# Attention values as the stationary operand, two heads on the column halves of TensorE, and softmax scaling after the product

## The chip, the cores and the metric

The kernel runs on one NeuronCore of a Trainium2 chip. The metric is the device time of one execution in microseconds (us). The kernel before took 1717.87 us, the median of 3 runs (1717.59 to 1725.1).

## What is computed

One layer of a streaming encoder for two inputs, a prompt of 1024 tokens and a sample of 64 tokens with 512 cached ones, all in fp32. The part that matters here is the token mixer:

```python
s = (einsum("bqhd,bkhd->bhqk", qn, k_nope) + einsum("bqhd,bkd->bhqk", qr, kr_all)) * mla_scale
w = softmax(where(mask, s, -1e30), axis=-1)            # 8 latent heads ("M")
mla = einsum("bqhk,bkhd->bqhd", w, v_mla)
...
w = where(mask, exp(log_beta + after), 0)              # 4 stick-breaking heads ("S")
sb = einsum("bqhk,bkhd->bqhd", w, sv_all)
...
mix = concatenate([mla, ret, sb], axis=-1) @ w_o       # 512 + 256 + 256 columns
```

Every head has 64 value columns. `ret` are four retention heads, computed apart. Ahead of the mixer stand the modulation, the norm and the input projection; behind it the output projection, the gated MLP with its convolution and a last norm.

## The kernel before

The mixer works on nine tiles of queries: tile 0 is the sample (64 rows, five blocks of keys, the last of 64 keys), tiles 1 to 8 are the prompt (128 rows; tile n has n blocks of 128 keys). Each tile has twelve units, one per head, in the order `S0 M0 M1 S1 M2 M3 S2 M4 M5 S3 M6 M7` (`KINDS`). The program on every engine is a loop over steps, one unit per step, written out by hand, with semaphores between the engines. In step t, TensorE (`@block.tensor`) does in this order:

- `scores(t)`: query times key (L2072 for M with 96 contraction rows, L2076 for S with 64), up to 1024 columns in two PSUM banks.
- `weigh` of the unit that was transposed one step earlier (L2121): for each block of 128 keys one product, whose stationary operand is the transposed probabilities `pT` (keys x 128 queries) and whose moving operand is the values (keys x 64). The result is 128 queries x 64 value columns in PSUM.
- `transposes` of the unit two steps back (M) or five steps back (S): blocks of the probabilities are turned by TensorE (L2101), up to four to a "piece" in bank 4 or 5, and ScalarE copies each piece into `pT` (`copy_piece`, L1176). A piece waits for the copy of the piece two before it, since two banks take turns. `PIECES` and `ORDER` number the pieces.
- one of twelve steps of the `front` of the next tile (the projections of queries, keys and values, their transposes and the retention products; L1984 to L2046). Tile 8 has no front beside it.

VectorE takes the row maxima (L1603), and in `head_output` it inverts one head's row sum (L1639) and writes the scaled result into `mixtok`, the tile's rows with 1024 columns (L1641), or copies it for S (L1645). ScalarE exponentiates (L1136) and runs the four passes of the S heads (L1148 to L1156). Five steps after a tile's last unit (`MIX_STEP` 17) two pieces "X" turn all eight 128-column blocks of `mixtok` (L2092), ScalarE copies them into `mixT` (L1169), and SyncE stores the tile in one DMA of 512 KB (L724). Tile 8 is copied straight into `mix_raw`, which the output projection (L2152) reads after ScalarE and VectorE have split it into two parts (L1226, L1686).

## Time and profile before

| | |
|---|---|
| median of 3 runs | 1717.87 us |
| the profiled execution: own time / span | 1719.77 / 1718.1 us |
| TensorE busy, share of the span | 1643.7 us, 96% |
| VectorE / ScalarE / GpSimd busy | 1067.6 / 608.7 / 170.5 us |
| mean granted TensorE clock | 0.978 |
| mixer, from the first score to the first product of the output projection | about 358 to 798 us |

The span is what the profiler's records cover; the execution's own time is 1.7 us longer. Busy time of TensorE counts each product to its modelled end, so that neighbours overlap; how closely products follow one another is read from start to start. PE is TensorE's products, PEld its loads of stationary operands, DVE VectorE, ACT ScalarE, POOL GpSimd, SP SyncE. An fp32 product stands in the trace as two records, each with its own load: the program's "x7" is "x14" there. Transposes are one record.

### The profile page before, as it was taken

The numbers are of one execution on the slowest core, as the hardware profiler recorded it, in microseconds if no ns is written. First come the engines' busy times: TensorE is split into PE (matmuls) and PEld (weight loads), VectorE is DVE, ScalarE is ACT, GpSimd is POOL, SyncE is SP. The second block draws the span as 40 slices with busy tenths as digits, with TensorE's granted clock in tenths as the row PEclk, the third lists the DMA queues.
The fourth block names the chain that finished last, engine by engine and source line by source line (L and its number), as shares of the span: only waits on it lengthen the run. The fifth ranks groups of instructions, "written<-read, shape, count | busy, mean of one in ns | idle before, by whom it ended". The sixth has DMA issues, their size and how long they took to land.

```text
span 1718.1 us, 27404 instructions
## 1 busy us (share of the span) xinstructions
PE 1643.7 (96%) x9986; PEld 1483.6 (86%) x9986; DVE 1067.6 (62%) x2325; ACT 608.7 (35%) x1199; POOL 170.5 (10%) x226
## 2 busy tenths in 40 slices
PE   6899999989999999998998999999999999999996
PEld 3599999646766777778998999999999999999996
DVE  3776655447676767666236665666666666665657
ACT  4621000236566667576135222222222222222213
POOL 0011111313222221111200000000000000000000
PEclk9899999979898999999999999999999999999999
DMA  9555555511111110035101111111111111111003
GB/s 332 195 155 160 173 161 167 178 37 42 61 48 48 49 48 5 13 124 197 50 26 48 39 50 37 37 61 37 49 37 39 59 37 49 37 47 51 12 1 117
DMA packets 114221, 133.61 MB, mean 78 GB/s; under 512 B 14954, under 2 KB 91545, under 8 KB 112793
## 3 DMA queue, kind: packets, MB, share of 16 engines
q1 hardware_dynamic: 110809, 121.76, 22.2%
q0 software_dynamic: 3328, 10.73, 1.8%
q8 instruction: 53, 0.87, 0.2%
q14 instruction: 31, 0.25, 0.0%
HBM read 107.47 MB, written 27.23 MB: 78 GB/s over the span
## 4 chain that ended last, share of the span: by engine, by line
PE 87%; ACT 5%; DVE 4%; issue 3%; DMA 0%; SPq 0%; ACTq 0%; DVEq 0%
PE psum L2152 34%; PE psum L2216 15%; PE psum L1918 11%; PE psum L2121 6%; PE psum L2072 3%; PE psum L2101 3%; PE psum L2076 2%; PE psum L2004 2%; PE psum L1946 1%; PE psum L1951 1%; PE psum L1822 1%; PE psum L1984 1%; DVE h_lo L1440 1%; ACT pT L1176 1%; PE psum L1844 1%
## 5 line engine op out<-in xcount | busy, mean ns | idle before, releaser
L2152 PE MATMUL psum<-act_hi,wt_parts 128*128 128x362 f32 (+1 forms) x2496 | 614.6, 328 | 9.4 <-DVE act_lo L1440 5.2
L1758 DVE SCALAR_TENSOR_TENSOR residual<-psum,mod,residual 128x364 f32<-128x364 f32 (+2 forms) x704 | 299.5, 493 | 257.6 <-PE psum L2216 257.6
L2152 PEld LDWEIGHTS psum<-act_hi,wt_parts 128*128 128x128 f32 x2496 | 441.1, 189 | 12.1 <-issue 6.8
L2152 PE MATMUL psum<-act_lo,wt_parts 128*128 128x362 f32 (+1 forms) x1248 | 408.1, 327 | 0.0
L2216 PE MATMUL psum<-u_hi,wt_parts 128*128 128x362 f32 (+1 forms) x1056 | 263.1, 330 | 3.0 <-issue 3.0
L2152 PEld LDWEIGHTS psum<-act_lo,wt_parts 128*128 128x128 f32 x1248 | 235.2, 188 | 0.0
L2216 PEld LDWEIGHTS psum<-u_hi,wt_parts 128*128 128x128 f32 x1056 | 188.0, 189 | 3.3 <-issue 3.3
L2216 PE MATMUL psum<-u_lo,wt_parts 128*128 128x364 f32 (+1 forms) x528 | 174.5, 330 | 0.0
L1918 PE MATMUL psum<-w_hi,h_hi 128*128 128x308 f32 x512 | 158.2, 309 | 2.7 <-DVE h_lo L1440 2.1
L1918 PE MATMUL psum<-w_lo,h_hi 128*128 128x308 f32 x512 | 156.7, 306 | 0.0
L1918 PE MATMUL psum<-w_hi,h_lo 128*128 128x308 f32 x512 | 156.1, 305 | 0.0
L1278 ACT ACTIVATE u_hi<-u_val 128x362 fp32r<-128x362 f32 (+1 forms) x66 | 33.4, 508 | 291.0 <-DVE u_val L1741 291.0
L1257 ACT ACTIVATE a_ext<-psum 128x364 f32<-128x364 f32 (+1 forms) x88 | 32.1, 392 | 224.9 <-PE psum L2152 224.9
L2121 PEld LDWEIGHTS psum<-v_mla,pT 128*128 128x128 f32 (+1 forms) x656 | 80.6, 190 | 32.1 <-issue 20.1
L1650 DVE TENSOR_TENSOR wt_parts<-wt_raw,wt_parts 128x1024 fp32r<-128x1024 f32 x74 | 91.0, 1232 | 21.7 <-ACT wt_parts L1197 21.7
L1176 ACT ACTIVATE pT<-psum 128x512 f32<-128x512 f32 (+3 forms) x156 | 69.3, 476 | 98.5 <-PE psum L2101 98.3
L1918 PEld LDWEIGHTS psum<-w_hi,h_hi 128*128 128x128 f32 x512 | 97.1, 190 | 4.8 <-DVE h_lo L1440 2.5
L2216 PEld LDWEIGHTS psum<-u_lo,wt_parts 128*128 128x128 f32 x528 | 100.3, 190 | 0.0
L1918 PEld LDWEIGHTS psum<-w_hi,h_lo 128*128 128x128 f32 x512 | 96.8, 189 | 0.0
L1918 PEld LDWEIGHTS psum<-w_lo,h_hi 128*128 128x128 f32 x512 | 96.8, 189 | 0.0
L2121 PE MATMUL psum<-v_mla,pT 128*128 128x64 f32 (+1 forms) x656 | 82.1, 271 | 12.9 <-ACT pT L1176 10.5
L2072 PE MATMUL psum<-kT,qT 96*128 96x512 f32 (+4 forms) x224 | 86.4, 498 | 1.2 <-DVE zsb L1617 1.2
(236 smaller groups left out, 2221.3 us busy)
## 6 DMA issues: line engine op xcount, KB each, us to landing
wt_raw<-in_w_up SPq DMA_DIRECT2D x44, 512.0 KB, 3.9
ada_raw<-in_w_ada SPq DMA_DIRECT2D x32, 512.0 KB, 3.9
wt_raw<-in_w_down SPq DMA_DIRECT2D x22, 512.0 KB, 4.4
w_raw<-in_w_in SPq DMA_DIRECT2D x16, 616.0 KB, 5.5
z_scratch<-z_out POOLq DMA_DIRECT2D x64, 154.0 KB, 3.1
z_in<-z_scratch SPq DMA_DIRECT2D x8, 1232.0 KB, 5.3
ada_first<-in_w_ada SPq DMA_DIRECT2D x16, 512.0 KB, 11.6
xT_scratch<-xT SPq DMA_DIRECT2D x1, 4352.0 KB, 18.4
```

The costliest lines, as they stand in the source:

```text
L1176: last = act.activation(pT[:, wn % 4, :len(blocks), :r], src[:, :len(blocks), :r], ACT.Copy)\
L1278: act.activation(u_hi[:, slot, a:b], u_val[:, c % 2, :b - a], ACT.Copy).then_inc(s_uh, 1)
L1650: dve.tensor_tensor(wt_lo[:, slot], wt_raw[:, raw], wt_hi[:, slot].bitcast(F32), ALU.subtract)\
L1758: last = dve.scalar_tensor_tensor(out=res[:, d, a:b], in0=bank[4 + q % 4][:, a - CHUNKS[c][0]:b - CHUNKS[c][0]], scalar=mod[:, 40 + d, whi ...
L1918: last = pe.matmul(out[:r, 0:ZG], hh[:, k, P * t:P * t + r], ww[:, slot, k, :], start=(k == 0 and m == 0), stop=(k == KT - 1 and m == 2))
L2004: last = pe.matmul(b7[:r, 0:384], qnT[:, k, :r], w_uq[:, k, 384 * (s - 2):384 * (s - 1)], start=(k == 0), stop=(k == 2))
L2072: last = pe.matmul(out, qT[:QD, slot, h, :r], kT[:QD, h, first + a:first + b], start=True, stop=True)
L2076: last = pe.matmul(out, sqT[lo:lo + 64, slot, h // 2, :r], skT[lo:lo + 64, h // 2, first + a:first + b], start=True, stop=True)
L2101: last = pe.transpose(out[:size, P * k:P * k + r], src[:, col - first:col - first + size], ident[:r, :r])
L2121: last = pe.matmul(bank[pv_bank(v)][:r, 64 * (v % 8):64 * (v % 8) + 64], pT[:size, W_NO[x] % 4, k % 4, :r], vals, start=(k == 0), stop=(k ...
L2152: last = pe.matmul(out[:, :b - a], ww[:, slot, P * k:P * k + P], aa[:, k, a:b], start=(k == 0 and m == 0), stop=(k == KT - 1 and m == 2))
L2216: last = pe.matmul(bank[4 + q % 4][:, :b - a], ww[:, ring, P * d:P * d + P], uu[:, slot, a:b], start=(m == 0), stop=(m == 2))
```

## The change

- `plan_pairs` joins heads 2p and 2p+1 of a kind. A pair is weighed in one step, the one after its second head's transposes: the steps with a `weigh` are 2, 3, 5, 8, 9 and 11 of every twelve, six in place of twelve.
- In `weigh` the operands change places. The stationary operand is the values of one head (keys x 64 columns), the moving one `pT` (keys x 128 queries). The first head of the pair goes to PSUM partitions 0 to 63, the second to 64 to 127, block by block in turn. The result is already transposed: 128 rows (two heads) x 128 queries.
- The inverse row sum now belongs to a column, not to a partition. `invert_sums` inverts two heads' sums in one instruction; a new piece "R" of two products spreads them (stationary: the inverse broadcast to 64 columns; moving: the identity), one on each column half. ScalarE copies it to `spread`, and VectorE multiplies it into the result (`pair_output`). R stands at the end of steps 1, 4, 7 and 10 of every twelve, behind the M pieces of that step.
- `pair_output` writes straight to `mixT` (or `mix_raw` in tile 8). The pieces X shrink to the two retention blocks (`MIX_STEP` 6), and `mixtok` to 256 columns.
- `pT` has eight slots in place of four; `mixT` is stored in seven smaller DMAs per tile, each waiting for its part; `rope_a` is gone, and `oc`, `oc2`, `gate` and `junk` move in SBUF.
- The program ends two steps earlier (112 in place of 114), and ScalarE starts the split once the last pair is written.

```diff
-MIX_STEP = 17
+MIX_STEP = 6
 ADA_AT = {1: 5, 2: 5, 3: 5, 4: 5, 5: 4, 6: 4, 7: 4}
...
+def plan_pairs():
+
+    out = {}
+    for n in range(NTILE):
+        for kind, heads in (("M", H_MLA), ("S", H_SB)):
+            for h in range(0, heads, 2):
+                units = tuple(12 * n + KINDS.index((kind, x)) for x in (h, h + 1))
+                out[units[1] + T_LAG[kind] + 1] = (n, kind, h // 2, units)
+    return [(step, *out[step]) for step in sorted(out)]
+
+
+PAIRS = plan_pairs()
...
         if rest == 0 and 0 <= n < NTILE:
-            out += [("X", n, 0), ("X", n, 1)]
+            out += [("X", n, 0)]
+        if PAIR_AT.get(step + 1) in M_PAIR:
+            out += [("R", PAIR_AT[step + 1], 0)]
         steps[step] = out
     return steps
...
+            def store_pair(v):
+                _, n, kind, p, _ = PAIRS[v]
+                sp.wait_ge(s_o, v + 1)
+                if n < NTILE - 1:
+                    store_mix(n, mix_block(kind, p), 1)
...
+                if kind == "R":
+                    r, free = rows_of(PAIRS[i][1]), [v for v in M_PAIR if M_PAIR[v] == M_PAIR[i] - 2]
+                    if free:
+                        act.wait_ge(s_o, free[0] + 1)
+                    act.activation(spread[:, M_PAIR[i] % 2, :r], src[:, 0, :r], ACT.Copy).then_inc(s_pt, 1)
+                    return
+                n, slot = UNITS[i][0], piece_slot(kind, i, j)
                 r = rows_of(n)
                 blocks = key_blocks(n)[4 * j:4 * j + 4]
-                if wn >= 4:
-                    act.wait_ge(s_pv, wn - 3)
-                last = act.activation(pT[:, wn % 4, :len(blocks), :r], src[:, :len(blocks), :r], ACT.Copy)\
+                free = pair_before(n, kind, UNITS[i][2] // 2)
+                if free is not None:
+                    act.wait_ge(s_pv, free + 1)
+                last = act.activation(pT[:, slot, :len(blocks), :r], src[:, :len(blocks), :r], ACT.Copy)\
                     if blocks[-1][1] == P else None
                 if last is None:
                     if len(blocks) > 1:
-                        act.activation(pT[:, wn % 4, :len(blocks) - 1, :r], src[:, :len(blocks) - 1, :r], ACT.Copy)
-                    last = act.activation(pT[:LS, wn % 4, len(blocks) - 1, :r], src[:LS, len(blocks) - 1, :r], ACT.Copy)
+                        act.activation(pT[:, slot, :len(blocks) - 1, :r], src[:, :len(blocks) - 1, :r], ACT.Copy)
+                    last = act.activation(pT[:LS, slot, len(blocks) - 1, :r], src[:LS, len(blocks) - 1, :r], ACT.Copy)
                 last.then_inc(s_pt, 1)
 
             def split_hi(n3, raw, slot, first=False):
...
 
-            def head_output(i):
-                n, kind, h = UNITS[i]
-                r, v = rows_of(n), PV_NO[i]
-                nb = len(key_blocks(n))
-                o = bank[pv_bank(v)][:r, 64 * (v % 8):64 * (v % 8) + 64]
+            def invert_sums(v):
+
+                _, n, kind, p, units = PAIRS[v]
+                r, u = rows_of(n), count_units("M", units[0])
+                dve.wait_ge(s_p, u + 2)
+                dve.reciprocal(inverse[:r, (u // 2) % 2, :], rowsum[:r, u % 4:u % 4 + 2, 0]).then_inc(s_nd, 1)
+
+            def pair_output(v):
+
+                _, n, kind, p, _ = PAIRS[v]
+                r, b = rows_of(n), mix_block(kind, p)
+                dve.wait_ge(s_pv, v + 1)
+                if n == NTILE - 1:
+                    dve.wait_ge(s_ret, NTILE)
+                    dve.wait_ge(s_fp, 12 * NTILE)
+                    dve.wait_ge(s_fA, read_a(NTILE, 0))
+                    out = mix_raw[:, b, LP - P:LP]
+                else:
+                    if n:
+                        dve.wait_ge(block_stored(b), 16 * n)
+                    out = mixT[:, b, :r]
+                result = bank[pv_bank(v)][:, P * (v % 4):P * (v % 4) + r]
                 if kind == "M":
-                    j = count_units("M", i)
-                    dve.wait_ge(s_p, j + 1)
-                    ch.link(dve.reciprocal(rowsum[:r, j % 4, 1:2], rowsum[:r, j % 4, 0:1]))
-                    dve.wait_ge(s_pv, W_NO[kind, i, (nb + 3) // 4 - 1] + 1)
-                    dve.tensor_scalar(mixtok[:r, n % 2, 64 * h:64 * h + 64], o, rowsum[:r, j % 4, 1:2], None,
-                                      ALU.mult).then_inc(s_o, 1)
+                    pieces_done(dve, ("R", v, 0))
+                    dve.tensor_tensor(out, result, spread[:, M_PAIR[v] % 2, :r], ALU.mult).then_inc(s_o, 1)
                 else:
-                    dve.wait_ge(s_pv, W_NO[kind, i, (nb + 3) // 4 - 1] + 1)
-                    dve.tensor_copy(mixtok[:r, n % 2, 768 + 64 * h:832 + 64 * h], o).then_inc(s_o, 1)
+                    dve.tensor_copy(out, result).then_inc(s_o, 1)
 
             def split_lo(n3, raw, slot):
 
...
                 if 0 <= step < len(UNITS):
                     (row_max if UNITS[step][1] == "M" else stick_logits)(step)
-                for x in PIECES.get(step - 1, []):
-                    if x[0] != "X" and x[2] == 0:
-                        head_output(x[1])
+                if step in PAIR_AT:
+                    pair_output(PAIR_AT[step])
                 if 0 <= step - 2 < len(UNITS) and UNITS[step - 2][1] == "S":
                     stick_sums(step - 2)
                 if s == 0 and 0 < m <= NTILE:
...
-                        pe.wait_ge(s_o, 12 * (i + 1))
-                    for k in range(4):
-                        last = pe.transpose(out[:, P * k:P * k + r],
-                                            mixtok[:r, i % 2, P * (4 * j + k):P * (4 * j + k) + P], ident[:r, :r])
+                    pe.wait_ge(s_ret, i + 1)
+                    for k in range(2):
+                        last = pe.transpose(out[:, P * k:P * k + r], mixtok[:r, i % 2, P * k:P * k + P], ident[:r, :r])
+                elif kind == "R":
+                    r, m = rows_of(PAIRS[i][1]), M_PAIR[i]
+                    pe.wait_ge(s_nd, m + 1)
+                    for a in range(2):
+                        last = pe.matmul(out[64 * a:64 * a + 64, 0:r], inverse[:r, m % 2, a:a + 1].broadcast_to([r, 64]),
+                                         ident[:r, :r], start=True, stop=True)
                 else:
                     n = UNITS[i][0]
                     r, u = rows_of(n), count_units(kind, i)
-                    pe.wait_ge(s_p if kind == "M" else s_w, u + 1)
+                    if kind == "M":
...
                     pe.wait_ge(s_sv, 80 if n < 5 else 96)
                 blocks = key_blocks(n)
                 for k, (_, size, tile_) in enumerate(blocks):
-                    x = (kind, i, k // 4)
                     if k % 4 == 0:
-                        pieces_done(pe, x)
-                    vals = v_mla[:size, tile_, 64 * h:64 * h + 64] if kind == "M" else \
-                        sv[:size, tile_, 64 * h:64 * h + 64]
-                    last = pe.matmul(bank[pv_bank(v)][:r, 64 * (v % 8):64 * (v % 8) + 64], pT[:size, W_NO[x] % 4, k % 4, :r],
-                                     vals, start=(k == 0), stop=(k == len(blocks) - 1))
-                    if k % 4 == 3 or k == len(blocks) - 1:
-                        last.then_inc(s_pv, 1)
+                        pieces_done(pe, (kind, units[0], k // 4))
+                        pieces_done(pe, (kind, units[1], k // 4))
+                    for a, i in enumerate(units):
+                        h = UNITS[i][2]
+                        vals = v_mla[:size, tile_, 64 * h:64 * h + 64] if kind == "M" else \
+                            sv[:size, tile_, 64 * h:64 * h + 64]
+                        last = pe.matmul(bank[pv_bank(v)][64 * a:64 * a + 64, P * (v % 4):P * (v % 4) + r], vals,
+                                         pT[:size, piece_slot(kind, i, k // 4), k % 4, :r],
+                                         start=(k == 0), stop=(k == len(blocks) - 1))
+                last.then_inc(s_pv, 1)
 
             for step in range(-12, STEPS):
                 m, s = divmod(step + 12, 12)
                 if 0 <= step < len(UNITS):
                     scores(step)
-                for x in PIECES.get(step - 1, []):
-                    if x[0] != "X" and x[2] == 0:
-                        weigh(x[1])
+                if step in PAIR_AT:
+                    weigh(PAIR_AT[step])
                 for x in PIECES.get(step, []):
                     transposes(x)
                 if m == 0:
```

TensorE in tile 4 (four blocks of keys), its steps 1 and 2: scores of M0 and M1, and what stands between them, before:

```order
L2072 MATMUL psum<-kT,qT 128x512 [waits softmax_exp_written]
L2121 MATMUL psum<-v_mla,pT 128x64 [waits piece_copied,head_output_written]
L2121 MATMUL psum<-v_mla,pT 128x64 x3
L2101 MATMUL psum<-ident_sb,prob 128x128 [waits softmax_exp_written,piece_copied]
L2101 MATMUL psum<-ident_sb,prob 128x128 x3
L2004 MATMUL psum<-w_uq_sb,qnT 128x384 [waits front_bank_read_by_scalar,front_bank_read_by_vector]
L2004 MATMUL psum<-w_uq_sb,qnT 128x384 x2
L2072 MATMUL psum<-kT,qT 128x512 [waits stick_logits_copied]
L2121 MATMUL psum<-v_mla,pT 128x64 [waits piece_copied,head_output_written]
L2121 MATMUL psum<-v_mla,pT 128x64 x3
```

The same two steps now (L2153 are the scores, L2210 `weigh`, L2189 the transposes, L2176 the piece R, L2085 the front's product with `w_uq`):

```order
L2153 MATMUL psum<-kT,qT 128x512 [waits softmax_exp_written]
L2189 MATMUL psum<-ident_sb,prob 128x128 [waits softmax_exp_written,piece_copied]
L2189 MATMUL psum<-ident_sb,prob 128x128 x3
L2176 MATMUL psum<-ident_sb,inverse 64x128 [waits pair_row_sums_inverted,piece_copied]
L2176 MATMUL psum<-ident_sb,inverse 64x128
L2085 MATMUL psum<-w_uq_sb,qnT 128x384 [waits front_bank_read_by_scalar,front_bank_read_by_vector]
L2085 MATMUL psum<-w_uq_sb,qnT 128x384 x2
L2153 MATMUL psum<-kT,qT 128x512 [waits stick_logits_copied]
L2210 MATMUL psum<-pT,v_mla 64x128 [waits piece_copied,head_pair_written]
L2210 MATMUL psum<-pT,v_mla 64x128 x7
L2189 MATMUL psum<-ident_sb,esb 128x128 [waits stick_weights_written,piece_copied]
L2189 MATMUL psum<-ident_sb,esb 128x128 x3
```

The four products of one head in each step are gone; eight products of two heads stand in the second step only, and the two of R stand between the transposes and the front in the first.

The last steps of TensorE's mixer (tile 8), before:

```order
L2072 MATMUL psum<-kT,qT 128x512 x2
L2121 MATMUL psum<-v_mla,pT 128x64 x8
L2101 MATMUL psum<-ident_sb,esb 128x128 x8
L2121 MATMUL psum<-sv,pT 128x64 x8
L2101 MATMUL psum<-ident_sb,prob 128x128 x8
L2121 MATMUL psum<-v_mla,pT 128x64 x8
L2101 MATMUL psum<-ident_sb,prob 128x128 x8
L2121 MATMUL psum<-v_mla,pT 128x64 x8
L2101 MATMUL psum<-ident_sb,esb 128x128 x8
L2121 MATMUL psum<-sv,pT 128x64 x8
L2092 MATMUL psum<-ident_sb,mixtok 128x128 x8
```

and now:

```order
L2176 MATMUL psum<-ident_sb,inverse 64x128 x2
L2153 MATMUL psum<-kT,qT 128x512 x2
L2210 MATMUL psum<-pT,v_mla 64x128 x16
L2189 MATMUL psum<-ident_sb,esb 128x128 x8
L2189 MATMUL psum<-ident_sb,prob 128x128 x16
L2176 MATMUL psum<-ident_sb,inverse 64x128 x2
L2210 MATMUL psum<-pT,v_mla 64x128 x16
L2189 MATMUL psum<-ident_sb,esb 128x128 x8
L2210 MATMUL psum<-pT,sv 64x128 x16
```

The closing transposes of `mixtok` are gone. Behind the last scores, five `weigh` of one head each have become three of a pair.

## Rows read from the trace of the kernel before

**Rows 1.** The page, parts 1 and 2: busy time, and the 40 slices of the span.

```profile
PE 1643.7 (96%) x9986; PEld 1483.6 (86%) x9986; DVE 1067.6 (62%) x2325; ACT 608.7 (35%) x1199; POOL 170.5 (10%) x226
...
PE   6899999989999999998998999999999999999996
...
PEclk9899999979898999999999999999999999999999
```

**Rows 2.** Windows: tiles 1, 4 and 7, first score to first score of the next.

```profile
core 0: us, PE busy (x) PEld busy (x) DVE busy (x) ACT busy (x) POOL busy (x), PEclk, DMA share, GB/s
407.60:436.60 29.00, 25.91 (x188) 20.00 (x187) 23.04 (x83) 19.05 (x71) 10.01 (x16) 1.00 0.20 63
...
512.60:560.30 47.70, 44.91 (x240) 32.25 (x239) 32.03 (x87) 29.59 (x68) 11.70 (x15) 0.89 0.13 43
...
665.70:726.60 60.90, 59.70 (x373) 45.39 (x372) 40.51 (x85) 40.21 (x74) 10.19 (x7) 1.00 0.03 10
```

**Rows 3.** Waits of PE, 366 to 800 us: total us, times, longest.

```profile
PE psum L2121 <- ACT pT L1176: 11.2, 16, 1.4
...
PE psum L2092 <- ACT pT L1176: 1.9, 5, 0.6
PE psum L2121 <- DVE mixtok L1641: 1.8, 1, 1.8
```

**Rows 4.** Timeline of PE in tile 7: start us, us, instruction, count.

```profile
704.84 0.60 PE L1984 MATMUL psum<-ident_sb,qtok 128*96 128x128 f32 x4
705.28 1.67 PE L2072 MATMUL psum<-kT,qT 96*128 96x512 f32 x4
706.78 1.67 PE L2121 MATMUL psum<-v_mla,pT 128*128 128x64 f32 x14
708.29 0.93 PE L2101 MATMUL psum<-ident_sb,esb 128*128 128x128 f32 x7
709.06 0.60 PE L1984 MATMUL psum<-ident_sb,qtok 128*96 128x128 f32 x4
709.59 1.77 PE L2076 MATMUL psum<-skT,sqT 64*128 64x512 f32 x4
711.29 1.77 PE L2121 MATMUL psum<-sv,pT 128*128 128x64 f32 x14
712.90 0.93 PE L2101 MATMUL psum<-ident_sb,prob 128*128 128x128 f32 x7
```

**Rows 5.** The same stretch, loads of stationary operands, around the S scores.

```profile
709.59 0.29 PEld L2076 LDWEIGHTS psum<-skT,sqT 64*128 64x128 f32 x2 [0.18 <-issue]
...
711.29 1.64 PEld L2121 LDWEIGHTS psum<-sv,pT 128*128 128x128 f32 x14 [0.54 <-issue]
```

**Rows 6.** Timeline of PEld in tile 0, 389.17 to 389.56 us: loads 64 wide.

```profile
389.10 0.55 PEld L2121 LDWEIGHTS psum<-v_mla,pT 128*64 128x64 f32 x8
```

**Rows 7.** Groups of the mixer, 358 to 797 us: count, busy us, mean ns, idle.

```profile
L1641 DVE TENSOR_SCALAR mixtok<-psum,rowsum 128x64 f32<-128x64 f32 (+1 forms) x72 | 20.4, 283 | 13.2 <-PE psum L2121 10.5 <-DVE rowsum L1639 0.2
...
L1639 DVE RECIPROCAL rowsum<-rowsum 128x1 f32<-128x1 f32 (+1 forms) x72 | 10.9, 152 | 0.0
...
L1645 DVE COPY mixtok<-psum 128x64 f32<-128x64 f32 (+1 forms) x36 | 7.7, 213 | 5.4 <-PE psum L2121 5.4
```

**Rows 8.** Timeline of the mixer's end.

```profile
792.63 1.97 PE L2121 MATMUL psum<-sv,pT 128*128 128x64 f32 x16 [0.34 <-ACT pT L1176]
794.63 0.23 DVE L1645 COPY mixtok<-psum 128x64 f32<-128x64 f32 x1 [2.83 <-PE psum L2121]
...
795.67 1.08 ACT L1169 ACTIVATE mix_raw<-psum 128x512 f32<-128x512 f32 x2 [2.70 <-PE psum L2092]
...
796.87 1.30 ACT L1226 ACTIVATE act_hi<-mix_raw 128x364 fp32r<-128x364 f32 x3
```

**Rows 9.** Windows at the lower clock, in tile 0 and in tile 4.

```profile
363.20:380.30 17.10, 15.96 (x49) 8.04 (x50) 7.75 (x15) 8.18 (x19) 2.84 (x3) 0.50 0.27 90
...
520.20:530.50 10.30, 10.30 (x36) 7.35 (x36) 6.29 (x13) 5.36 (x14) 1.27 (x1) 0.50 0.35 133
```

More of the change, by code:

```diff
@@ L222 @@
 PIECE_NO = {x: q for q, x in enumerate(ORDER)}
[L223 to L227 removed]
 PV_LAST_LOW, PV_FIRST_TAIL = 12 * 5 - 2, 12 * 8 + 1
 def pv_bank(v):
[L233 to L234 removed]
+    step, _, kind, _, _ = PAIRS[v]
+    if kind == "S" and 12 <= step <= PV_LAST_LOW:
         return 1
[L236 removed]
+    if kind == "S" and step >= PV_FIRST_TAIL:
         return 7
@@ L1134, in softmax_exp @@
                 if j >= 4:
[L1135 removed]
+                    act.wait_ge(s_nd, (j - 4) // 2 + 1)
                 act.activation(prob[:r, j % 3, :w], score_bank(i, w)[:r], ACT.Exp, bias=maxes[:r, j % 2, 1:2],
@@ L2100, in transposes, with weigh @@
                     for k, (col, size, _) in enumerate(key_blocks(n)[4 * j:4 * j + 4]):
-                        last = pe.transpose(out[:size, P * k:P * k + r], src[:, col - first:col - first + size],
-                                            ident[:r, :r])
+                        to, of = out[:size, P * k:P * k + r], src[:, col - first:col - first + size]
+                        last = pe.transpose(to, of, ident[:r, :r])
                 last.then_inc(s_tr, 1)
-            def weigh(i):
-                n, kind, h = UNITS[i]
-                r, v = rows_of(n), PV_NO[i]
+            def weigh(v):
+                _, n, kind, p, units = PAIRS[v]
+                r = rows_of(n)
                 if pv_user_before(v, pv_bank(v)) is not None:
```

117 lines of the change are left out of this document (72 added, 45 removed).

## The prediction

> **What bounds the kernel now.** I read the page first: TensorE is busy 96% of the span, and only a few of the forty slices fall under 9 tenths [rows 1]. The change touches the mixer alone, 358 to 798 us, so I cut that into its tiles. Tile 7 takes 60.9 us with PE busy 59.7 and no DMA to speak of; ScalarE is busy 40.2 and VectorE 40.5 of them. Tile 4 has PE busy 44.9 of 47.7, tile 1 25.9 of 29.0 [rows 2]. TensorE bounds the large tiles; in the small ones part of the time is a chain of engines answering each other. The named waits of PE in the whole mixer are small, 11.2 us for ScalarE's copies being the largest [rows 3]. So the question is what the new order costs TensorE, product by product.
>
> **How dear a `weigh` is.** In tile 7, with seven blocks, the M scores start at 705.28 and 706.78 is the first of the values' products, 708.29 the first transpose: 1.51 us for 14 records [rows 4], 0.108 us a record, 0.216 a block and head. The seven transposes behind it take 0.77 us, 0.110 each [rows 4]. A product streams 64 columns there and a transpose 128, yet both follow at the same pace, so the 128-wide load sets it. Scores of 896 columns take 1.50 us in two passes: 0.84 us per 1000 columns and pass, so 128 fp32 columns stream in 0.107. A load 64 wide is cheaper: in tile 0 eight of them span 0.55 us, and with a single record of 0.14 taken off, seven intervals of 0.058 [rows 6].
>
> **How dear a change of tile shape is.** The S scores use 64 contraction rows, the M scores 96. Against the M case, the step ahead of the S scores is longer by 0.09 (709.06 to 709.59 beside 704.84 to 705.28), the scores themselves by 0.20 (1.70 beside 1.50) and the values behind by 0.10 (1.61 beside 1.51) [rows 4]: 0.39 us for going to the half array and back. The load records say why: the first load behind each change starts with its product, and is not hidden under the one before [rows 5]. I take 0.20 us a change where a 128-wide load follows, and 0.15 where the load is 64 wide (0.20 less 0.110, plus 0.058). The Trainium skill, TensorEngine Tiling (Array Packing), Key Properties, says that changing the tiling mode drains TensorE; by that rule, the trace agrees. It speaks against this change, which puts two changes around every new `weigh` and every R.
>
> **The sum on TensorE.**
>
> 1. *Products with the values.* Twelve heads in tiles 1 to 8 have 1+2+...+8 = 36 blocks each: 216 pairs of blocks at 2 x 0.216 = 0.432 us. Now each is four records of 128 streamed columns and four 64-wide loads. The trace shows no two products on different column halves. From both sides: if the halves run side by side, the loads set 4 x 0.058 = 0.232, a gain of 0.200 each, 43 us in all; if they run one after the other, 4 x 0.107 = 0.43, no gain. I take the first, because the pace in rows 4 and 6 was always that of the load, which was hidden under the product before, and the halves share neither operand nor partitions. Tile 0 loads 64 wide already and streams 64 columns: 0.058 a record before and after, nothing.
> 2. *Changes of shape.* In tiles 1 to 8, four `weigh` a tile follow M scores (0.15 + 0.20 new) and two follow S scores, where one change was there before at 0.20 (0.15 new in balance): 32 x 0.35 + 16 x 0.15 = +13.6 us. The last product of each streams 0.107 before the drain, where the next load was hidden before: 48 x 0.05 = +2.4.
> 3. *R.* 36 times: in 0.15, four records 0.27, out 0.20 = 0.62: +22 us. In the five-to-eight-block tiles R is a third piece and must wait for the copy of the first; the only such place now is X, and there PE waited 1.9 us in 5 times [rows 3], 0.38 each. Some 0.1 is the drain anyway: 16 x 0.3 = +4.8.
> 4. *X* loses six of eight transposes in nine tiles: 54 x 0.110 = -5.9.
> 5. *The end.* After the last write of `mixtok` (794.63 + 0.23) came transposes and copies until ScalarE split at 796.87 [rows 8]: 2.0 us that now vanish, and the last stick-breaking head's chain is met by three `weigh`, not five. I take -3 beyond item 4.
> 6. *Fewer waits.* Half as many `weigh` wait for ScalarE's copy, with more room before each (11.2 and 1.8 us now [rows 3]): -5. In tiles 1 to 4, where PE is not alone the bound, I hide a quarter of the 17 us that items 2 and 3 add there: -4.
>
> Together -43 + 13.6 + 2.4 + 22 + 4.8 - 5.9 - 3 - 5 - 4 = -18. I give 3 us of it back to ScalarE and VectorE: in tile 7 they are at 66% now, and the same work in some 56 us puts them above 70%, where queues begin to show. **-15 us.**
>
> **The other engines.** VectorE drops 72 inversions at 0.152, 72 scalings at 0.283 and 36 copies at 0.213 [rows 7], 39 us, for 36 inversions, 36 multiplications and 18 copies of 128 columns (0.35 at the outside): some 24 us. That is off the path in the large tiles. ScalarE gets 36 copies of R and loses half of X: even. R needs both row sums inverted at the step's start; behind VectorE's place for it wait the row maxima of that step, but both exponentials belong to units two and three steps back, and the transposes just before R wait for the same ones: nothing. What is queued behind R on PE (the front, the next scores) moves by its 0.62 alone. SyncE issues seven stores a tile in place of one; its next load of `z` now stands behind the store of step 11, a moment before the retention output that it waits for anyway: nothing. Before VectorE overwrites a block of `mixT`, twelve steps have passed.
>
> Against its own time (1719.8; span 1718.1) that gives 1704.8, and against the median of 1717.9, which is 1.9 lower, **1703 us**. Half a percent, 8.6 us, is about what a measurement of this kernel can tell from no change.
>
> **Rivals.**
>
> - *B, the halves overlap in part.* The loads may stay one ahead: the load for a product starts when the product before it starts. Within a block the order is first half twice, second half twice; the first pass of the second half then waits 0.058 for its load, the second pass waits 0.107 for the first, and so on: 0.107 + 0.058 + 0.107 + 0.058 = 0.33 us a pair of blocks. The gain falls to 216 x 0.10 = 22 us and R costs 3 more: 6 us above the median, 1724. For it: every load in rows 4 and 5 stands one ahead and never two. The Trainium skill, TensorE: Matmul & The Clock Gate, Part 3, says a load overlaps running products only when its row group differs, and column halves share row groups; rows 4 show loads hidden under products of the same rows, so here the trace does not agree as far as it goes.
> - *C, slower: the halves take turns.* 4 x 0.107 a pair, no gain in item 1, R at 0.8: +43 + 4 on my sum, 1749 us. It decides from the point where a pair of blocks costs over 0.37 us. For it: two 128-wide streams at once appear nowhere in this trace. The Trainium skill, TensorEngine Tiling, Key Properties and When to Use Tiling, states that tiles load and multiply in parallel and names just this swap of operands with two column tiles; that is forecast A, and no row here shows it.
> - *D, TensorE gains and nothing comes of it.* ScalarE's passes and VectorE's scans become the chain, or the granted clock dips more. It already halves in stretches, 17.1 us in tile 0 and 10.3 in tile 4 with PE busy throughout [rows 9]; every ten more such us cost five. Time as before, 1718, half a percent to either side.
>
> **How the numbers follow.** A has 0.48: as its terms are good to some 8 us, 0.39 of that is faster by over half a percent, 0.09 within. B 0.22: 0.13 within, 0.08 slower, 0.01 faster. C 0.22, all slower. D 0.08, mostly within. Faster 0.41, same 0.28, slower 0.31. A alone would be 1692 to 1712. The range must reach into C, which holds more than may be left out: 1690 to 1749.
>
> **What would show it.** In tile 7, a pair's `weigh` of 28 records: 1.6 us start to start if A, 2.3 if B, 3.0 if C. The first load behind each change unhidden, R some 0.6 us. Tile 7 at 55 us, tile 1 at 30 or more. PE waiting 0.3 us for a copy ahead of R from tile 5 on. ScalarE splitting 5 us or so sooner after the last scores. I am wrong if records of the two halves do not start closer than 0.107 us, if tile 7 shortens but PE then waits for VectorE or ScalarE, or if the lower clock spreads.

## The result, and the profile after

The changed kernel takes **1801.5 us** (median of 4 runs, 1794.2 to 1808.2), the kernel before, run beside it, 1717.7 (4 runs). The ratio is 1.048, with a 95% interval of 1.043 to 1.053: slower by 84 us, and outside the range that I gave (1690 to 1749). The ratios of the later runs are each to runs of the kernel before on the same chip, with medians of 1717.7 to 1721.2 us; where two experiments were measured on different chips, a difference of their times is good to 3 or 4 us.

The page after, parts 1 and 2, for [rows 1]:

```profile
PE 1658.9 (92%) x10076; PEld 1456.6 (81%) x10076; DVE 1056.1 (59%) x2235; ACT 613.7 (34%) x1226; POOL 171.6 (10%) x226
...
PE   6899999878888878787899899999999999999996
...
PEclk9999999976789998988899999999999999999999
```

Windows after, for [rows 2]: tiles 1, 4 and 7, first score to first score of the next; the last row is tile 8, to the output projection (same columns).

```profile
413.90:457.80 43.90, 34.95 (x197) 25.04 (x196) 20.95 (x73) 19.90 (x74) 10.44 (x16) 0.69 0.14 46
544.60:591.30 46.70, 41.16 (x250) 25.41 (x250) 30.77 (x76) 29.60 (x71) 11.80 (x15) 0.93 0.14 45
719.90:788.30 68.40, 56.71 (x382) 37.58 (x381) 39.92 (x75) 40.85 (x77) 10.20 (x7) 0.95 0.03 9
788.30:878.70 90.40, 70.20 (x437) 45.19 (x436) 42.22 (x69) 47.76 (x79) 12.49 (x5) 0.79 0.27 87
```

Waits of PE after, 366 to 880 us, for [rows 3]:

```profile
PE psum L2176 <- ACT pT L1242: 55.4, 20, 4.9
PE psum L2176 <- DVE inverse L1704: 25.8, 14, 3.5
...
PE psum L2171 <- ACT pT L1242: 2.1, 5, 0.6
```

In tile 7, PE is busy for 3 us less than before and yet the tile takes 7.5 us more. PE was idle for 1.2 us of it, and is now for 11.7. L2176 is the piece R: PE waits in 34 of its 36 places, 81.2 us in all, 20 times for ScalarE's copy (2.8 us each) and 14 times for VectorE's inverse (1.8 each). The granted clock has fallen too: 0.69 in tile 1 and 0.79 in tile 8, where it was 1.00 in both. In the stretches at 0.50, TensorE runs at 1.2 GHz instead of 2.4.

One of the waits for ScalarE, in tile 7. Timeline of PE (start us, us, instruction, count, idle time before it and what ended it):

```profile
742.78 0.93 PE L2189 MATMUL psum<-ident_sb,prob 128*128 128x128 f32 x7
746.92 0.44 PE L2176 MATMUL psum<-ident_sb,inverse 128*64 128x128 f32 x4 [3.21 <-ACT pT L1242]
747.29 2.20 PE L2085 MATMUL psum<-w_uq_sb,qnT 128*128 128x384 f32 x6
749.33 1.67 PE L2153 MATMUL psum<-kT,qT 96*128 96x512 f32 x4
750.92 1.75 PE L2210 MATMUL psum<-pT,v_mla 128*64 128x128 f32 x28
752.61 0.98 PE L2189 MATMUL psum<-ident_sb,esb 128*128 128x128 f32 x7
```

The same time on ScalarE:

```profile
742.63 0.95 ACT L1203 ACTIVATE esb<-zsb 128x896 f32<-128x896 f32 x1
743.61 0.95 ACT L1204 ACTIVATE esb<-esb 128x896 f32<-128x896 f32 x1
744.59 0.95 ACT L1205 ACTIVATE esb<-esb 128x896 f32<-128x896 f32 x1
745.45 0.93 ACT L1211 ACTIVATE esb<-esb 128x896 f32<-128x896 f32 x1
746.29 0.96 ACT L1242 ACTIVATE pT<-psum 128x512 f32<-128x512 f32 x2
```

R is the third piece of its step and needs the PSUM bank of the first, which ScalarE must empty. The transposes ended at 743.7. But the copy stands in ScalarE's queue behind the three passes of `stick_log` and the one of `stick_weights`, 3.7 us, which are issued in the same step. They fall in steps 1, 4, 7 and 10 of every twelve, just those at whose end R stands. All 20 waits for ScalarE are in tile 0 and tiles 5 to 8, with five or more blocks.

The 14 waits for VectorE are at the R of tiles 1 to 4. One of them, on PE and then on VectorE:

```profile
482.05 0.39 PE L2189 MATMUL psum<-ident_sb,prob 128*128 128x128 f32 x2
485.62 0.52 PE L2176 MATMUL psum<-ident_sb,inverse 128*64 128x128 f32 x4 [3.18 <-DVE inverse L1704]
```

```profile
483.04 0.89 DVE L1594 TENSOR_SCALAR zqn<-z_in,rs 128x384 f32<-128x384 f32 x1 [1.47 <-ACT rs L1131]
483.85 0.95 DVE L1595 SCALAR_TENSOR_TENSOR lat<-z_in,rs,g_kv_sb 128x256 f32<-128x256 f32 x1
484.72 0.68 DVE L1634 TENSOR_TENSOR att<-psum,decayT_sb 128x512 f32<-128x512 f32 x1
485.32 0.15 DVE L1704 RECIPROCAL inverse<-rowsum 128x2 f32<-128x2 f32 x1
```

The exponentials were done when PE transposed. The inversion is the first thing of VectorE's step, but it stands behind three instructions of the step before, for the next tile, which VectorE had not finished; the first of them had itself waited for ScalarE.

**Where the 83 us went.** From the single records and the slices of the granted clock I split each mixer (first score to first product of the output projection) into three: PE's idle time, its time at half clock, and its own work, which is what is left when idle time and half of the busy time at half clock are taken off. The figures of the experiments are put here as well. Each row is one profiled execution. Because own work is what is left over, such a split always adds up; what it shows is how large the parts are.

| kernel | mixer | PE idle | at half clock | own work at 2.4 GHz |
|---|---|---|---|---|
| before | 439.6 | 28.1 | 44.4 | 390.1 |
| changed | 522.8 | 94.2 | 163.8 | 355.0 |
| e1 R in the next step | 432.3 | 47.5 | 72.9 | 350.3 |
| e2 no R | 424.0 | 47.9 | 71.7 | 342.1 |
| e3 R of ones | 496.3 | 79.2 | 133.1 | 356.3 |
| e4 R first | 503.3 | 90.0 | 122.9 | 358.7 |
| e5 e1, R one transpose | 443.0 | 51.4 | 95.6 | 347.2 |
| e6 e5, copies first | 440.5 | 50.8 | 90.1 | 347.3 |
| e7 halves in turn | 476.7 | 47.0 | 96.9 | 383.8 |
| e8 copies first | 461.7 | 59.5 | 99.0 | 356.9 |
| e9 e1, R one product | 443.1 | 51.8 | 81.9 | 352.7 |
| e10 weigh two later | 432.8 | 44.7 | 83.2 | 347.6 |
| e11 e10, R wide | 445.0 | 51.9 | 85.3 | 353.8 |
| e12 e11, cheap inverse | 458.5 | 46.3 | 126.3 | 352.2 |
| e13 change, waits filled | 474.6 | 52.9 | 47.8 | 399.8 |
| e14 the same, half as much | 497.4 | 68.1 | 110.6 | 376.5 |
| e15 e10, waits filled | 427.8 | 33.5 | 51.2 | 369.2 |

So the change did save TensorE 35 us of work. Against that stand 66 us of idle time, and 52 us by the lower clock (half of 147.2 us busy at half clock, less half of 42.8 before): -35 + 66 + 52 = +83.

The other rows. VectorE in the mixer after, for [rows 7]:

```profile
L1723 DVE TENSOR_TENSOR mixT<-psum,spread 128x128 f32<-128x128 f32 (+1 forms) x32 | 9.1, 284 | 8.5 <-PE psum L2210 8.0
L1704 DVE RECIPROCAL inverse<-rowsum 128x2 f32<-128x2 f32 (+1 forms) x36 | 5.5, 152 | 0.0
L1725 DVE COPY mixT<-psum 128x128 f32<-128x128 f32 (+1 forms) x16 | 4.4, 275 | 1.6 <-PE psum L2210 1.6
```

The mixer's end after, for [rows 8]:

```profile
875.03 1.97 PE L2210 MATMUL psum<-pT,sv 128*64 128x128 f32 x32
878.67 0.57 PE L2240 MATMUL psum<-act_hi,wt_parts 128*128 128x364 f32 x2 [1.68 <-DVE act_lo L1767]
```

From the start of the last `weigh` to the output projection it is 3.6 us, where it was 5.5 (792.63 to 798.1).

### The profile page after: what moved, and what is told of

It is laid out like the page before. It is cut to its first block, busy times and chain, and to the rows that moved or that the text cites. A ratio compares the mean times of both kernels' runs of the same rounds, so it can differ in the third digit from the quotient of the medians.

```text
span 1800.8 us, 27614 instructions
## 1 busy us (share of the span) xinstructions
PE 1658.9 (92%) x10076; PEld 1456.6 (81%) x10076; DVE 1056.1 (59%) x2235; ACT 613.7 (34%) x1226; POOL 171.6 (10%) x226
## 4 chain that ended last, share of the span: by engine, by line
PE 83%; ACT 7%; DVE 5%; issue 4%; DMA 0%; SPq 0%; POOL 0%; ACTq 0%; DVEq 0%
PE psum L2240 33%; PE psum L2304 15%; PE psum L1999 11%; PE psum L2210 4%; PE psum L2153 3%; PE psum L2085 2%; PE psum L2189 2%; PE psum L2157 2%; PE psum L2065 1%; PE psum L2032 1%; PE psum L2027 1%; PE psum L2176 1%; PE psum L1903 1%; ACT esb L1204 1%; ACT esb L1203 1%
## 5 line engine op out<-in xcount | busy, mean ns | idle before, releaser
L1344 ACT ACTIVATE u_hi<-u_val 128x362 fp32r<-128x362 f32 (+1 forms) x66 | 33.5, 509 | 290.9 <-DVE u_val L1822 290.9
L2153 PE MATMUL psum<-kT,qT 96*128 96x512 f32 (+4 forms) x224 | 102.7, 577 | 0.9 <-issue 0.9
L1999 PEld LDWEIGHTS psum<-w_lo,h_hi 128*128 128x128 f32 x512 | 96.9, 189 | 0.0
L2176 PE MATMUL psum<-ident_sb,inverse 128*64 128x128 f32 (+1 forms) x144 | 19.2, 351 | 81.2 <-ACT pT L1242 55.4
L948 POOL TENSOR_TENSOR esb<-zsb,esb 64x576 f32<-64x576 f32 (+8 forms) x36 | 51.9, 1442 | 377.2 <-DVE esb L1697 362.0
```

Source lines behind the costliest of these rows:

```text
L948: pool.tensor_tensor(esb[:r, j % 2, :w], zsb[:r, j % 2, :w], esb[:r, j % 2, :w], ALU.subtract)\
L1999: last = pe.matmul(out[:r, 0:ZG], hh[:, k, P * t:P * t + r], ww[:, slot, k, :], start=(k == 0 and m == 0), stop=(k == KT - 1 and m == 2))
L2153: last = pe.matmul(out, qT[:QD, slot, h, :r], kT[:QD, h, first + a:first + b], start=True, stop=True)
L2176: last = pe.matmul(out[64 * a:64 * a + 64, 0:r], inverse[:r, m % 2, a:a + 1].broadcast_to([r, 64]), ident[:r, :r], start=True, stop=True)
```

## The experiments

### R moved, left out, freed of one wait

**e1** moves R from the end of its step into the next one, behind its scores and ahead of `weigh`.

```diff
-        if PAIR_AT.get(step + 1) in M_PAIR:
-            out += [("R", PAIR_AT[step + 1], 0)]
+        if PAIR_AT.get(step) in M_PAIR:
+            out.insert(0, ("R", PAIR_AT[step], 0))
...
+                for x in PIECES.get(step, []):
+                    if x[0] == "R":
+                        transposes(x)
                 if step in PAIR_AT:
                     weigh(PAIR_AT[step])
...
```

> The piece R moves from the end of its step to the head of the next one, behind the scores and ahead of weigh; nothing else. Theory Q (queue): in the changed kernel PE waits at R 55 us for ScalarE's copy of the step's first piece, which stands in ScalarE's queue behind three passes of the next stick-breaking head and an exponential, and 26 us for VectorE's inverses; the idle stretches then halve the clock (163 us at the lower clock in the mixer against 44 before). With R one step later both are long done: the waits at R fall below 5 us, the lower clock goes back to under 70 us, and the time to 1695 to 1712 us. Rival K (clock and shape): the products on half the columns and the changes of shape themselves lower the clock and cost the time; then the waits at R go, but the time stays above 1750 us.

Measured: 1716.8 us (10 runs), ratio 0.998 (0.995 to 1.001): 85 us under the changed kernel, though above the 1712 that I had given as the most. The wait at R shrank from 81.2 us to 21.6, not under 5, as its group shows:

```profile
L2176 PE MATMUL psum<-ident_sb,inverse 128*64 128x128 f32 (+1 forms) x144 | 16.7, 312 | 21.6 <-ACT pT L1242 12.3 <-DVE inverse L1704 9.3
```

Tile 7 of e1 (window, as in rows 2) takes what the forecast had said, 55 us:

```profile
664.80:720.30 55.50, 52.98 (x383) 36.20 (x382) 39.93 (x75) 39.92 (x77) 10.20 (x7) 1.00 0.04 10
```

Tiles 2 to 7 take 268 us together in e1 and 290 before, but tiles 0 and 1 take 91.5 instead of 78.1. PE is idle there for 10.0 us, 6.9 before, but 49.1 us are at half clock, 17.1 before, so that the lower clock alone gives back most of that. So R's place is the loss of the changed kernel, and without it the change is worth no more than a draw.

**e2** leaves R out, and the latent heads are written without their scaling.

> R is left out, and the results of the latent heads are not scaled by their row sums (part of the computation is missing); the value products stay as changed. Theory Q: without R there is no wait of that kind, about 1680 to 1700 us, some 15 to 20 us under the kernel with R one step later (36 R at about half a microsecond). Rival K: the value products alone keep the clock low, over 1740 us.

Measured: 1703.1 us (2 runs), ratio 0.989 (0.985 to 0.993), 14 us under e1. The two mixers differ by 8.3 us, 8.2 of them own work, which prices R at 0.23 us for each of 36. The profiled executions differ by 15.5 us, and the 7 us outside the mixer, where the two programs are the same, are no price of R.

**e3** keeps R in the changed kernel's place, but spreads a constant one, so that it does not wait for VectorE (the result is then not scaled).

```diff
-                    pe.wait_ge(s_nd, m + 1)
...
-                        last = pe.matmul(out[64 * a:64 * a + 64, 0:r], inverse[:r, m % 2, a:a + 1].broadcast_to([r, 64]),
+                        last = pe.matmul(out[64 * a:64 * a + 64, 0:r], ones[:r, 0:64],
```

> R stays where the change put it, but spreads a constant 1 in place of the inverses and so does not wait for VectorE (the scaling is missing from the result). It splits the two waits. Theory Q: the 26 us for VectorE go, the 55 us for ScalarE's copies stay, perhaps a little more: 1765 to 1785 us. If VectorE's wait were the root and ScalarE's a consequence of it, under 1740 us.

**e4** puts R ahead of the other pieces of its own step (`out.insert(0, ...)` in place of `out +=`).

> R stays in its step but stands ahead of the step's pieces, not behind them. Theory Q: it no longer waits for the copy of a piece of its own step, but in tiles 5 to 8 the step's second piece now needs R's bank, whose copy stands behind the same passes in ScalarE's queue, so the wait moves from R to the transposes there and the time stays at 1780 to 1810 us. If it were only R's place as third piece, the time would fall under 1750 us.

**e8** leaves TensorE's order as in the changed kernel and turns ScalarE's: the exponential, `stick_weights`, then the copies, and `stick_log` last.

```diff
-                for lag, kind, do in ((1, "M", softmax_exp), (1, "S", stick_log), (4, "S", stick_weights)):
...
+                passes((1, "M", softmax_exp), (4, "S", stick_weights))
                 for x in PIECES.get(step, []):
                     copy_piece(x)
+                passes((1, "S", stick_log))
```

> The changed kernel with R where the change put it, and only ScalarE's order changed: pieces are copied ahead of the three passes of the stick-breaking head. Theory Q, from the other side: the 55 us that R waits for the copy shrink to some 10, the wait for VectorE's inverses stays at 26 or grows: 1735 to 1770 us. If ScalarE's queue were not the reason, 1795 to 1805.

Measured: e3 1779.3 us (2 runs), e4 1784.9 (2), e8 1741.4 (2). Their waits at R, in this order (e3, e4, e8):

```profile
PE psum L2175 <- ACT pT L1242: 54.9, 20, 4.9
```

```profile
PE psum L2176 <- DVE inverse L1704: 50.9, 27, 3.7
PE psum L2189 <- ACT spread L1234: 26.8, 16, 2.5
```

```profile
PE psum L2180 <- DVE inverse L1708: 35.8, 21, 3.5
PE psum L2180 <- ACT pT L1242: 11.5, 13, 3.4
```

All three lie within what was expected. The two waits are separate. Without VectorE's (e3) ScalarE's is untouched, and 22 us come back; idle time falls by 15 us and not by 26, since the `weigh` behind now waits 9.6 us for copies, in 8 places. R first in its step (e4) trades ScalarE's wait for a longer one on VectorE, and the pieces behind R now wait for R's own copy. In e8 ScalarE's wait falls from 55.4 to 11.5 us, and **60 us come back with no instruction of TensorE moved**: the copy's place in ScalarE's queue was the larger part of the loss. VectorE's wait grows to 35.8 us there, in 21 places in place of 14: where ScalarE's had come last, VectorE's now does.

### Do the column halves overlap?

**e7** is e1 with `weigh` doing all blocks of the first head, then all of the second.

> The kernel with R one step later, but weigh runs all blocks of the first head and then all of the second, so that products on the two column halves do not stand next to each other. If the halves run side by side only when their products alternate, each pair of blocks costs 0.43 us in place of 0.22: 216 x 0.21 = 45 us on PE, of which the waits in the small tiles hide some: 1740 to 1762 us. If interleaving is not what gives the overlap, the time stays within 5 us of 1717.

Measured: 1752.8 us (4 runs), ratio 1.018 (1.014 to 1.021), 36 us over e1 (34 by the two ratios); own work rises by 33.5. The `weigh` of seven blocks, e1 and then e7:

```profile
701.15 1.70 PE L2210 MATMUL psum<-pT,v_mla 128*64 128x128 f32 x28
```

```profile
730.11 2.86 PE L2210 MATMUL psum<-pT,v_mla 128*64 128x128 f32 x28
```

The same 28 records take 1.70 us in alternation and 2.86 in turn. In the single records of the changed kernel, the products of the two halves start 7 ns apart (751.085 and 751.092), the next two at 751.195 and 751.201, and so do their loads. That is 0.11 us for two records, one of each half, and 0.22 for a pair of blocks: full overlap, and only where neighbours in the order use different halves.

### Cheaper R

**e5** and **e9** are e1 with both inverses written 64 times each, so that R is one transpose (e5) or one product (e9), 128 wide, without halves; **e6** is e5 with e8's order on ScalarE.

> On the kernel with R one step later: R is one transpose 128 wide of the inverses, which VectorE writes out 64 times each (one instruction), in place of two products on the column halves. Four records, two changes of shape go, one record comes: by my terms 0.62 us a R less 0.11, in 36 R 18 us at most; where PE waits anyway, nothing. Theory Q: 1700 to 1712 us. If changes of shape cost nothing beyond what is hidden, the time stays at 1717 within 3 us.

Measured: e5 1722.4 us, ratio 1.000 (0.998 to 1.002); e6 1720.1, 1.000 (0.998 to 1.002); e9 1725.3, 1.002 (1.000 to 1.005; e5 and e6 12 runs each, e9 10). All three miss what I had hoped for, 1700 to 1712 us for e5 and e9 and 5 to 15 us under e5 for e6; none gains on e1. The own work of e5 is 3.1 us under e1's, but idle time is 3.9 and time at half clock 22.7 us over it. What I had not priced shows in VectorE's groups of e9 (e5's is the same):

```profile
L1704 DVE RECIPROCAL inverse<-rowsum 128x128 f32<-128x128 f32 (+1 forms) x36 | 33.8, 940 | 0.0
```

An inversion of 128 columns takes 940 ns, one of two columns 152: 28 us more on VectorE, ahead of the waits for it. That this is what cost e5 and e9 their gain is argued, not shown; e12 below does not bear it out.

### More distance

**e10** is e1 with `weigh` and R one more step later, so that the copies and the inverse have a step of their own.

```diff
-                out[units[1] + T_LAG[kind] + 1] = (n, kind, h // 2, units)
+                out[units[1] + T_LAG[kind] + 2] = (n, kind, h // 2, units)
...
-                if step + 1 in PAIR_AT and PAIRS[PAIR_AT[step + 1]][2] == "M":
-                    invert_sums(PAIR_AT[step + 1])
+                if step + 2 in PAIR_AT and PAIRS[PAIR_AT[step + 2]][2] == "M":
+                    invert_sums(PAIR_AT[step + 2])
...
```

> R one step later, and then every weigh with its R one step later still; the inverses are made when they were. Theory Q: R then has a whole step more for ScalarE's copies and VectorE's inverses. The 12 and 9 us that PE still waits at R, and 2.5 at weigh, fall under 3 us, the lower clock falls from 73 us towards the 44 of before, and the time is 1690 to 1705 us. If the small tiles are bound by a chain that does not go through R, the waits move to the scores and the time stays within 6 us of 1717.

Measured: 1713.9 us (8 runs), ratio 0.994 (0.992 to 0.996). PE waits 0.9 us at R in the whole mixer, and yet the gain that I had named, 1690 to 1705 us, did not come: idle time is 44.7 us and e1's was 47.5, because PE now waits elsewhere, 18.5 us ahead of transposes and 6.8 ahead of stick-breaking scores. **e11**, e10 with e9's R, takes 1726.3 (12 runs; 1.002, 1.000 to 1.004), where I had expected 1680 to 1705; **e12** inverts two columns and widens them by a copy:

> Edit: e10 (pairs weighed two steps later, R at the head of the step), and R is one product 128 wide, as in e11, but VectorE inverts only two columns (0.15 us) and a copy of its own widens them to 128 columns, in place of the 0.94 us inversion that e11 shows. Theory T (what e11 lost against e10 is VectorE's 36 x 0.79 = 28 us of longer inversions, and the change of shape around R has a price on TensorE): the copy costs some 0.2 us, VectorE's inversions and copies together under 15 us, R no longer runs on halves, so that M pairs have R and the change of shape to 128 wide behind it as before; 1711 us, 1706 to 1716, and 3 us under e10. Rival U (R's one product reads 128 wide at full price, 0.2 us, and the change of shape moves merely from R to the weigh behind it, so there is nothing to gain): as e10, 1714, 1711 to 1718. Rival V (the longer wait for the inverse, not the inversion's time, is what cost e11): 1722 or more.

```profile
L1706 DVE COPY inverse<-narrow 128x128 f32<-128x128 f32 (+1 forms) x36 | 13.0, 361 | 1.2
L1705 DVE RECIPROCAL narrow<-rowsum 128x2 f32<-128x2 f32 (+1 forms) x36 | 5.5, 152 | 0.0
```

Measured: 1736.4 us (6 runs), ratio 1.009 (1.006 to 1.012). Readings T and U are out. The time lies in V's range, but V's mechanism is not there: PE waits 0.9 us at R, as in e10. VectorE does need less, 18.5 us in place of 33.8. PE's idle time is 1.6 us over e10's and its own work 4.6. But 126 us of the mixer are at half clock, 43 more than in e10; the other executions bear that out, with 0.952 to 0.964 of the clock granted over the span in six, against 0.964 to 0.969 in e10's eight. That raised the question of what the lower clock follows.

### Is it idle time that brings the lower clock?

**e13** is the changed kernel, with 16 transposes of the identity ahead of R's wait in 25 places; their result is overwritten by the next `weigh`. **e14** has 8 in place of 16 (`FILL_COUNT`).

```diff
+                if kind == "R" and M_PAIR[i] in FILL:
...
+                    for _ in range(FILL_COUNT):
+                        pe.transpose(bank[pv_bank(i)][:, P * (i % 4):P * (i % 4) + r], ident[:r, :], ident[:r, :r])
                 if q >= 2:
                     pieces_done(pe, ORDER[q - 2])
```

> Edit: the changed kernel, with 16 transposes of the identity, whose result is overwritten by the next weigh, issued by TensorE just ahead of R's wait in 25 of the 36 places, those in which the changed kernel waits 1.96 us or more at R. They take 16 x 0.11 = 1.8 us at the full clock, less than the wait, so that ScalarE and VectorE answer as before and R starts when it did: TensorE is busy in some 44 of its 94 us of idle time, and nothing else changes. Theory T (TensorE's idle stretches bring the lower clock, and the lower clock is 52 of the 83 us that the mixer grew by): time at half clock in the mixer falls from 164 to 100 us or less, and the kernel takes 1760 to 1778. Rival U (the lower clock has another cause, such as the halves' products or the sum of work, and idle time has no part in it): half clock 150 us or more, 1795 to 1812, or more by the stretches at half clock in which 16 transposes outlast the wait.

> Edit: as e13, with 8 transposes in place of 16, 0.9 us at the full clock. Theory T: between the changed kernel and e13, half clock some 130 us, 1780 to 1792. Rival U: as the changed kernel, 1795 to 1808.

Measured: e13 **1749.6 us** (4 runs), ratio 1.019 (1.015 to 1.024); e14 1776.7 (4 runs), 1.031 (1.027 to 1.036). The changed kernel's clock in forty slices stands above; here is e13's:

```profile
PEclk9999999987999999999999999999999999999999
```

and its waits at R:

```profile
PE psum L2184 <- ACT pT L1244: 25.2, 19, 3.2
PE psum L2184 <- DVE inverse L1706: 14.4, 14, 1.8
```

TensorE does 45 us more of work that nobody reads, and the kernel is 52 us faster (49 by the two ratios). Both times are below what I had given, 1760 to 1778 and 1780 to 1792. Time at half clock falls from 164 to 111 (e14) to 48 us (e13) as idle time falls from 94 to 68 to 53. From changed to e13, own work is up by 45, which is the 400 transposes at 0.11 us; idle time is down by 41; and busy time at half clock goes from 147 to 44, half of which is -52. So filling a wait costs about what it fills, and the gain is the clock's. Over the span 0.940 to 0.951 of the clock was granted in the changed kernel's four runs, and 0.970 to 0.980 in e13's. The rival, that the lower clock has nothing to do with idle time, is out.

**e15** is e10 with such transposes in 17 places where it still waits. The counts in its edit add up to 192, as in the trace, not to the 170 of the expectation.

> Edit: e10 with idle transposes of the identity, as in e13, issued by TensorE where e10 still waits over 0.9 us: 5 to 20 ahead of the transposes of eleven stick-breaking heads, 8 to 14 ahead of the front's transposes in six places, 170 in all, 19 us of some 25 us of idle time there. Nothing else changes. Theory T (idle time brings the lower clock): half clock in the mixer 83 to 60 us or less, the kernel 1703 to 1711, under e10 and under the kernel before. Rival U (only waits longer than those of e10, 2 to 3.5 us as in e13, matter to the clock, or e10's half clock comes with TensorE busy, as the 22 us at its start): no less half clock, 1713 to 1720, since some fills outlast their wait.

Measured: **1703.9 us** (6 runs), ratio 0.989 (0.986 to 0.992), the fastest version that computes the reference, within what was expected. Half clock is 51 us (83 in e10), idle time 33.5 (44.7), and own work is up by 22. The fillers, in their two kinds of places:

```profile
L2175 PE MATMUL psum<-ident_sb 128*128 128x128 f32 (+1 forms) x122 | 15.2, 276 | 0.0
L2075 PE MATMUL psum<-ident_sb 128*128 128x128 f32 x70 | 10.1, 300 | 11.0 <-DVE att L1636 6.3 <-DVE skT L1612 4.8
```

## Why the prediction was wrong

**The step that failed** is the price of the waits at R, in the paragraph on the other engines and in item 3. "R needs both row sums inverted at the step's start; [...] the transposes just before R wait for the same ones: nothing." The transposes wait for the exponential alone; R waits until VectorE comes to the inversion, behind its instructions of the step before, and that took 25.8 us in 14 places. And "R is a third piece and must wait for the copy of the first", 16 x 0.3 = 4.8 us: measured 55.4 us in 20 places (I had left out the four of tile 0, which has five blocks too). I took the price from X [rows 3], which waits 0.38 us. But there ScalarE stands idle when the pieces come: in tile 7 of the kernel before, the copies at 692.50 us had themselves waited 2.09 us for TensorE. In R's steps it has four passes of up to 0.95 us ahead of the copy. ScalarE runs `stick_log` and `stick_weights` in one of three steps, and the prediction did not set those steps beside R's. A wait is priced by the queue of the engine waited for, at the step where it stands, not by another wait for the same kind of copy. e8, which alters that queue alone, is the proof: 60 us. Two of the signs that I had named for being wrong came true, that PE waits for VectorE or ScalarE and that the lower clock spreads.

**The second failure** is in rival D, "the granted clock dips more [...] every ten more such us cost five". The rate is right, the size was held to no more than the gain (1718 us, at a chance of 0.08), and the link was missed: a wait costs its own length, and here half clock came with it. In the changed kernel 66 us of idle time came with 52 us by the clock; e13 shows that the second goes when the first is filled. The Trainium skill, TensorE: Matmul & The Clock Gate, Part 1, says that the clock is set by how busy TensorE has been recently; e13 agrees, half clock falling from 164 to 48 us as the waits were filled. [Rows 9] had misled me: there the clock is low with PE busy throughout.

**What was right.**

- *Item 1, the halves overlap.* Forecast A said 1.6 us for a `weigh` of 28 records, B 2.3, C 3.0: it is 1.69 (750.92 to 752.61). Before, two heads took 3.02. e7 gives products in turn, as rival C had them, and against e1 it costs the 36 us that C's item 1 was worth (43, less what waits hide); that its 1753 us stand so near to C's 1749 is luck, since e1 stands 14 us above the forecast. The Trainium skill, TensorEngine Tiling (Array Packing), Key Properties, says that tiles load and multiply in parallel; the trace agrees, with products of the two halves 7 ns apart. The Trainium skill, TensorE: Matmul & The Clock Gate, Part 3, says that a load overlaps running products only in another row group; the trace does not agree, since the loads of both halves, which use the same rows, start 7 ns apart under running products, and a pair of blocks still takes 0.22 us.
- *Items 2 to 4 were too dear.* By my sum, own work should have fallen by 11 us (-43 + 13.6 + 2.4 + 22 - 5.9); it fell by 35, and in e1 by 40. R takes 0.37 us start to start (746.92 to 747.29), not 0.62, and e2 prices it at 0.23 of own work. The scores ahead of a `weigh` take 1.59 us beside 1.51 ahead of transposes, 0.08 for the change of shape, not 0.15; the `weigh` itself takes 0.16 more than its seven pairs at 0.218 (1.53), 0.05 of it at its first product and 0.11 behind its last, where I had 0.20 for the change back and 0.05 for the last product.
- *Item 5*: the last `weigh` to the projection is shorter by 1.8 us; I had said 3. *Item 6*: the waits ahead of `weigh` did vanish (11.2 us before; none shows after, and the longest gap there is 0.12 us), but those at R took their place sevenfold.
- *The other engines*: VectorE's two new kinds cost 0.284 and 0.275 us, and the pair's inversion 0.152 [rows 7]; in all 21 us in place of 39, where I had 24. No wait of TensorE, VectorE or ScalarE in the mixer is for a DMA, so the seven stores a tile cost nothing that shows.
- *The rivals' sums.* B's 1724 us leaves out the 3 us given back to ScalarE and VectorE, and C's 1749 keeps them; on one footing B is 1727 us and C 1750. That changes no chance by much.

e1 is in effect what the forecast described, with R's waits much smaller: 1717, and not 1703, for 47 us of idle time in place of 28 and 73 us at half clock in place of 44. TensorE saved 40 us of own work there, of which idle time took 19 and the lower clock 13.

**What stays open.** Idle time is not all that moves the clock: e12 idles 1.6 us more than e10 and has 43 us more at half clock. In tile 0, PE is idle for 3.8 us both before and in e1, with 17.1 us at half clock before and 32.0 in e1 (one execution each). So a part of rival K, that the new products themselves lower the clock, is not ruled out for the small tiles. No run tells why. e8's order on ScalarE was not tried with e10, nor the fillers in the kernel before, so that part of what e15 gains might be had without the change.

## What to carry to other kernels

A new step on the engine that bounds the kernel must be placed by the queues of the engines that it waits for: list what they issue in that same step, and add it up. Count a wait of TensorE more than once: against the kernel before, each us of added idle time came with 0.5 to 1.3 us lost by the clock in the rows without fillers (2.1 in e12). That is an estimate from this kernel, not a rule. Where a wait can't be removed, try idle products in it (here up to 52 us). Two heads' products, each 64 columns of values wide, on the two column halves cost about as much as one head's did (1.69 us beside 1.51 for seven blocks), if the order alternates between the halves product by product.

## What was unexpected of the hardware

- Work that nobody needs made a kernel 52 us faster (e13 against the changed kernel), by the granted clock: 0.980 over the span in place of 0.947 in the profiled executions.
- Inverting 128 columns on VectorE takes 940 ns, and a copy to 128 columns 361; an inversion of two columns 152.
- The products of the two column halves start 7 ns apart and both their loads are hidden, in fp32: two records, one of each half, take 0.109 us, and one transpose of the same 128 columns took 0.110 [rows 4].
